# A mixed network of attention, gated linear attention and retention: GpSimd makes the low parts of the weights in the three mixed layers

## The reference

```python
# layer 1
h = rms_norm(x, norm1_g);  proj = h @ w_in
o_attn = dilated_attention(q, k, v, gq, gk)            # 3 groups of 8 heads, merged by their softmax sums
o_gla  = rms_norm(gated_linear_attention(p_q, p_k, p_v, log_a)) * silu(p_r)
x = x + (gate_0 * (o_attn @ w_attn_branch) + gate_1 * (o_gla @ w_gla_branch)) @ w_out
x = x + square(relu(rms_norm(x) @ w_ff_up)) @ w_ff_down
# layer 2: windowed attention with a sink, and neighbourhood attention with a bias table
x = x + concat(window_gqa(...), neighbourhood_attn(...)) @ w_out_e;   x = x + mlp(x)
# layer 3: retention forward and backward, group norm, silu gate
x = x + (silu(g) * group_norm(y_forward + y_backward)) @ w_out_o;     x = x + mlp(x)
```

## Time and profile before

| | us |
|---|---|
| median of 3 runs (2575.36 to 2576.57) | 2576.25 |
| the profiled execution | 2576.55 |
| its span, first to last instruction | 2574.8 |
| PE busy | 2485.3 |
| DVE busy | 1312.8 |
| ACT busy | 934.0 |
| POOL busy | 59.3 |

### The profile page before, as it was taken

One profiled execution on the slowest core, in us unless ns is written; L12 is line 12 of the kernel. 1 busy time (PEld: TensorE's weight loads), 2 busy tenths in 40 slices (PEclk: granted clock), 3 DMA queues, 4 the chain that ended last, 5 costly groups with the idle time before them and its releaser, 6 DMA issues.

```text
span 2574.8 us, 32784 instructions
## 1 busy us (share of the span) xinstructions
PE 2485.3 (97%) x12748; PEld 1949.0 (76%) x12748; DVE 1312.8 (51%) x2065; ACT 934.0 (36%) x1471; POOL 59.3 (2%) x131
## 2 busy tenths in 40 slices
PE   7999999887899999999999999999999999999999
PEld 5777777666788888876576888887677776788887
DVE  4555554665554334447656443345566455634433
ACT  5333453334423223345444332233223232423322
POOL 4000000000000000021000000000000000000000
PEclk9999999998999999999999999999999999999999
DMA  4222213111233333330112333333222221333222
GB/s 140 66 67 66 67 55 94 58 57 43 74 98 99 90 98 103 93 99 25 42 33 74 107 90 98 98 99 89 66 66 82 75 68 41 111 99 107 89 93 78
DMA packets 60640, 205.79 MB, mean 80 GB/s; under 512 B 7249, under 2 KB 7249, under 8 KB 60386
## 3 DMA queue, kind: packets, MB, share of 16 engines
q1 hardware_dynamic: 59760, 202.93, 26.2%
q10 hardware_dynamic: 754, 1.14, 0.1%
HBM read 201.94 MB, written 2.10 MB: 79 GB/s over the span
## 4 chain that ended last, share of the span: by engine, by line
PE 88%; DVE 6%; ACT 4%; issue 1%; POOL 1%; DMA 0%; POOLq 0%; DVEq 0%; ACTq 0%
PE psum L1409 75%; PE psum L1456 2%; PE psum L1492 1%; PE psum L1438 1%; PE psum L1449 1%; PE psum L1434 1%; PE psum L1514 1%; PE psum L1519 1%; PE psum L1484 1%; DVE stage L913 1%; PE psum L1537 0%; ACT tmp L602 0%; DVE arena L1067 0%; ACT tmp L604 0%; PE psum L1504 0%
## 5 line engine op out<-in xcount | busy, mean ns | idle before, releaser
L1409 PE MATMUL psum<-hhi,whi 128*128 128x512 f32 x1640 | 656.7, 400 | 18.1 <-POOL g_mask L501 8.9
L1409 PE MATMUL psum<-hlo,whi 128*128 128x512 f32 x1640 | 666.4, 406 | 0.0
L1409 PE MATMUL psum<-hhi,wlo 128*128 128x512 f32 x1640 | 653.4, 398 | 0.0
L1409 PE MATMUL psum<-uhi,whi 128*128 128x512 f32 x1392 | 555.3, 399 | 7.2 <-DVE hlo L953 2.5
L1409 PE MATMUL psum<-ulo,whi 128*128 128x512 f32 x1392 | 551.4, 396 | 0.0
L1409 PE MATMUL psum<-uhi,wlo 128*128 128x512 f32 x1392 | 547.3, 393 | 0.0
L882 DVE TENSOR_TENSOR wlo<-raw,whi 128x1024 fp32r<-128x1024 f32 (+1 forms) x399 | 465.4, 1167 | 56.1 <-ACT whi L847 29.1
L1409 PEld LDWEIGHTS psum<-hhi,whi 128*128 128x128 f32 x1640 | 313.5, 191 | 88.3 <-POOL g_mask L501 8.9
L1409 PEld LDWEIGHTS psum<-hhi,wlo 128*128 128x128 f32 x1640 | 313.8, 191 | 73.8 <-issue 9.5
L1409 PEld LDWEIGHTS psum<-hlo,whi 128*128 128x128 f32 x1640 | 314.3, 192 | 71.3 <-issue 9.1
L847 ACT CAST whi<-raw 128x1024 fp32r<-128x1024 f32 x190 | 199.6, 1051 | 351.9 <-PE psum L1409 351.9
(11 more groups left out here) (199 smaller groups left out, 1824.5 us busy)
## 6 DMA issues: line engine op xcount, KB each, us to landing
raw<-in_packed_dram SPq DMA_DIRECT2D x359, 512.0 KB, 3.6
raw<-in_packed_dram SPq DMA_DIRECT2D x40, 256.0 KB, 2.6
x<-in_xt_dram SPq DMA_DIRECT2D x8, 256.0 KB, 7.5
out_dram<-x SPq DMA_DIRECT2D x8, 256.0 KB, 2.0
arena<-in_near_bias_dram ACTq DMA_DIRECT2D x1, 1024.0 KB, 5.7
vec<-in_vec_dram ACTq DMA_DIRECT2D x1, 44.0 KB, 4.0
arena<-in_gla_gate_up_dram ACTq DMA_DIRECT2D x1, 32.0 KB
arena<-in_gla_gate_bias_dram ACTq DMA_DIRECT2D x1, 2.0 KB
```

The costliest lines, as they stand in the source:

```text
L1409: mm = pe.matmul(g, w[:, u % 4, k, :], v[:, k, :], start=n == 0, stop=n == 3 * kt - 1)
```

## The change

`split_lo` leaves the mixed layers of DVE. POOL runs it instead, for all units that DVE did in the steps of the three mixed layers and for the two units before the first step: 209 splits, 169 of 1024 columns and 40 of 512. DVE keeps the 142 rows (190 splits, some in loops) of the feed-forward layers. PE waits for `lo_done` as before, now counted up by two engines in turn; for that DVE waits for `lo_done` at the start of each feed-forward layer.

The masks of POOL become functions. `d_pick` is made right behind the constants, without its wait for the first norm. The others stand in a table by unit (`jobs`): at the step of that unit POOL first runs the mask, then the split of u+2. One level of `g_mask` stands at each of the units 2 to 6 of the first layer, the rest of it at unit 7, the dilated mask at 8, the windowed mask at unit 4 of the second layer and all 48 selects of the neighbourhood bias at unit 5.

The first lines that are taken out lie in the steps of the mixed layers, the added wait in the feed-forward layers, the last ones at the start of DVE.

```diff
+            def level_mask(i, m):
...
+            def own_mask():
...
+            def pick():
...
+            def dil_mask():
+                pool.wait_ge(mask_copied, 1)
...
+            def near_mask():
+                pool.wait_ge(rpb_in, 16)
+                within(near_first, near_bias[:, :, 64:256], 8, True)
...
+            def split_lo(u, kt):
+                if u in (first("l2"), first("l3")):
+                    pool.wait_ge(lo_done, u)
+                pool.wait_ge(hi_done, u + 1)
+                pool.tensor_tensor(wlo[:, u % 4, 0:kt, :], raw[:, u % 4, 0:kt, :], whi[:, u % 4, 0:kt, :].bitcast(F32),
+                                   ALU.subtract).then_inc(lo_done, 1)
+            pa = UNIT_OF["copy", "w_in", 0, PA]
+            jobs = {first("l1") + 2 + i: functools.partial(level_mask, i, m) for i, m in enumerate(HALVINGS[2:])}
+            jobs |= {first("l1") + 7: own_mask, first("l1") + 8: dil_mask, pa + 1: ones_row, first("l2") + 4: win_mask, first("l2") + 5: near_mask}
+            pick()
+            split_lo(0, KD)
+            split_lo(1, KD)
+            for name in ("l1", "l2", "l3"):
+                for u, _, _ in steps[name]:
+                    if u is None:
+                        continue
+                    if u in jobs:
+                        jobs[u]()
+                    if not (name != "l1" and u + 2 < first(name) + 2):
+                        split_lo(u + 2, units[u + 2][4])
+                if name == "l1":
+                    distances()
+                if name == "l2":
+                    ret_distance()
...
-                    if u is not None:
-                        split_lo(u + 2, kt=units[u + 2][4])
...
+                dve.wait_ge(lo_done, b + 2)
...
             for k in range(KD):
-                if k == 2:
-                    split_lo(0)
                 squares_after(0, k)
-            split_lo(1)
```

More of the change, by code:

```diff
@@ L1 @@
+import functools
 from contextlib import ExitStack
@@ L502, in _ @@
                                             pattern=[[2 * m, 16 // m], [0, m]], channel_multiplier=-1))
-            for j in range(4):
+            def own_mask():
+              for j in range(4):
                 r = g_mask[32 * j:32 * j + 32, 5, :]
@@ L559, in _ @@
-            within(near_bias, near_bias, 0, False)
-            pool.sem_inc(near_masked, 1)
-            pool.wait_ge(norm_lo, KD * (ORDER["ff1"] + 1))
-            pool.iota(r_dist, pattern=[[1, 7 * P]], base=-3 * P, channel_multiplier=-1,
-                      allow_small_or_imprecise_dtypes=True).then_inc(dist_ready, 1)
+            def pick():
+                done(pool.memset(d_pick, 0.0))
+                v = d_pick[0:4, :].rearrange("p (a b) -> p a b", b=4)
+                done(pool.affine_select(out=v, in_=v, compare_op=ALU.not_equal, fill=1.0, base=0,
+                                        pattern=[[0, P // 4], [-1, 4]], channel_multiplier=1))
+                pool.sem_inc(pick_ready, 1)
@@ new lines, in dil_mask @@
+            def dil_mask():
+                pool.wait_ge(mask_copied, 1)
+                for j in range(4):
+                    r = slice(32 * j, 32 * j + 32)
+                    v = d_bias[r, 0:P]
+                    done(pool.affine_select(out=v, in_=v, compare_op=ALU.is_ge, fill=NEG, base=-j, pattern=[[1, P]],
+                                            channel_multiplier=-4))
+                    v = d_bias[r, P:2 * P]
+                    done(pool.affine_select(out=v, in_=v, compare_op=ALU.is_ge, fill=NEG, base=j, pattern=[[-1, P]],
+                                            channel_multiplier=4))
+                    v = d_bias[r, 256:512].rearrange("p (g l) -> p g l", g=2)[:, :, 96:128]
+                    done(pool.affine_select(out=v, in_=v, compare_op=ALU.is_ge, fill=NEG, base=0, pattern=[[0, 2], [-1, 32]],
+                                            channel_multiplier=1))
+                pool.sem_inc(mask_ready, 1)
@@ new lines, in win_mask @@
+            def win_mask():
+                pool.wait_ge(dist_abs, 1)
+                for sign in (1, -1):
+                    done(pool.affine_select(out=win_dist, in_=win_dist, compare_op=ALU.is_ge, fill=-NEG, base=P - sign * P,
+                                            pattern=[[sign, 3 * P]], channel_multiplier=-sign))
+                pool.sem_inc(dist_pool, 1)
+            def near_mask():
+                pool.wait_ge(rpb_in, 16)
+                within(near_first, near_bias[:, :, 64:256], 8, True)
+                within(near_first[:, :, 128:192], near_first[:, :, 128:192], 24, False)
+                within(near_last, near_bias[:, :, 0:192], 0, False)
+                within(near_last[:, :, 0:64], near_last[:, :, 0:64], 0, True)
+                within(near_bias, near_bias, 0, True)
+                within(near_bias, near_bias, 0, False)
+                pool.sem_inc(near_masked, 1)
```

53 lines of the change are left out of this document (14 added, 39 removed).

## The result

| | before | after |
|---|---|---|
| median, us | 2575.81 (4 runs, 2575.01 to 2576.57) | 2612.36 (4 runs, 2610.43 to 2621.73) |
| ratio to before, 95% interval | | 1.0149 (1.0124 to 1.0174) |
| profiled execution, us | 2576.55 | 2621.73 |
| mean granted clock of the profiled execution | 0.986 | 0.979 |

The change makes the kernel 36.5 us slower, 1.5%. The profiled execution is the longest of the four; the others took 2610 to 2614 us at a clock of 0.982 to 0.984. Lines of the kernel after stand 52 further down in DVE's part (L913 is L965 now) and 47 further down in PE's (L1409 is L1456, L1602 is L1649).

A forecast was written before the change was run, and what follows sets the result against it. PE, busy 2485.3 of 2574.8 us, was taken to set the time. Terms -4.9 + 6.8 + 4 + 2.2 + 10.8 + 10.7 = +29.6 on 2576.55 us gave 2606 us, range 2580 to 2634.

The forecast's parts named there:

- start: Program start: early d_pick removes a 3.54 us wait and the half clock behind, split 1 costs +1.3; together -4.9 us.
- level masks, dilated attention: First layer: splits have two units of lead and miss L1007, so nothing; attention within -2 to +4 us.
- gla heads: Ahead of gla heads 1 to 3 and behind head 3: a split holds DVE's chain, 4 x 1.7 = +6.8 us.
- inside them: Inside the gla heads: splits meet DVE's differences and factors in about two of six units; +4 us, bounds -2 and +10.
- branch: Branch units: two splits hold L949 to L953, DVE's own split goes; 2 x 1.7 - 1.2 = +2.2 us.
- neighbourhood masks: Second layer: unit 7's split queues behind 48 selects; PE waits 8.4 us, then half clock 2.4; +10.8 us.
- retention: Retention heads: splits hold DVE's part 4 chain; 8.5 for five heads, 0.5, 0.8 and 0.9 for others; +10.7 us.
- rival without a hold: POOL does not hold DVE; only start and neighbourhood masks remain, +5.9, 2582 us; chance 0.17.
- rival "faster": The 48 selects end within 22 us, before PE needs unit 7; 2566 us; chance 0.06.
- dear input: The second input makes a POOL split 3.8 us and DVE's hold 3.5; +65, 2642 us; chance 0.14.
- head 4 has a split on the chain now: Retention head 4: a POOL split replaces the DVE split on the chain; 1.7 - 1.2 = +0.5 us.
- Freeing DVE of 209 splits gives PE almost nothing: Mixed layers: DVE's 1.23 us splits mostly lie beside PE's matmuls or ACT's later-ending gate functions, so almost no gain.

The follow-up runs named there:

- e4_all: After, with the edits of e2_near and e3_clear and POOL's split also held back behind part 11 of gla and the branch posts; 2569.16 us, ratio 0.9970.
- e2_near: After, with the neighbourhood bias loaded and its 48 selects run by POOL during the first feed-forward layer; 2604.21 us, ratio 1.0101 to before.
- e3_clear: After, with POOL's split waiting until DVE is through with part 4 of a retention head; 2589.31 us, ratio 1.0051 to before.
- e5_none: e2_near without any split in the mixed layers after the first four units, POOL only counting up (old low parts read); 2560.53 us, ratio 0.9950.
- e1_pick: The kernel before, with only d_pick made ahead of the level masks and all splits kept on DVE; 2570.49 us, ratio 0.9978.
- e8_near_clear: After, with the edits of e2_near and e3_clear but no added waits in gla and at the branch posts; 2581.38 us, ratio 1.0018 to before.
- e9_all_pieces: e4_all, with POOL's split cut into 128-column instructions from the third unit on; 2564.17 us, ratio 0.9957 to before.
- e10_all_256: e4_all, with POOL's split cut into 256-column instructions from the third unit on; 2568.67 us, ratio 0.9966 to before.
- e6_pieces: e2_near, with each POOL split cut into 8 or 4 instructions of 128 columns; 2577.53 us, ratio 1.0008 to before.

## Why the prediction came out right, and which steps did not

The forecast was 2606 us in a range of 2580 to 2634; 2612.4 was measured. Step by step, with the measured terms taken from the traces: PE's 12748 products are the same in every kernel, so each was matched with its like in the kernel before, and a row says how much PE lost in that stretch.

| us of the kernel before | terms | forecast | after | with the cause taken away |
|---|---|---|---|---|
| 0 to 60 | start | -4.9 | -4.9 | |
| 60 to 480 | level masks, dilated attention | 0 | -1.9 | |
| 480 to 740 | gla heads 6.8, inside them 4, branch 2.2 | +13.0 | +15.0 | -0.1 (e4_all) |
| 1145 to 1240 | neighbourhood masks | +10.8 | +12.4 | +0.8 (e2_near) |
| 1240 to 1761 | none | 0 | +0.7 | |
| 1761 to 2300 | retention | +10.7 | +23.9 | -3.3 (e3_clear) |
| sum | | +29.6 | +45.2 | |

The profiled execution of after is the longest of its four; by the medians the change costs 36.5 us, and no trace shows where the other executions are shorter.

**The mechanism was right.** A split holds a DVE instruction until it ends, PE pays where that is on its chain, and the selects hold the split of unit 7. Each of the three losses goes when its cause is taken away, as the last column shows. The rival without a hold falls with the 2.50 us of L1124; the rival "faster" falls with 30.6 us of selects, where it needed 22; the dear input, 3.8 us a split, falls with 2.44.

**The split was mis-sized**, 2.44 instead of 2.0 us, and the hold 2.07 instead of 1.7. The fault was not to take a line up to 1024 columns: the shortest splits, 0.445, 0.717, 1.267 and 2.34 us for 128, 256, 512 and 1024 columns, lie on a line too, with the same 0.17 us at its foot. It was to take the selects' 1.77 ns a column, where the subtraction costs 2.12. The Trainium skill (GPSIMD Engine Reference, section 3.1) would have given 2.25 by half of its 2048-column figure, an estimate that is closer than my line. The gla wait answers to it: 8.92 where I forecast 8.6. The +4 for splits inside the heads was too much: e4_all leaves them there and comes to -0.1 us in that stretch, e5_none, without any, to -2.3, so they are worth some 2 us. The waits ahead of the heads and at the branch, 9.0 forecast, were worth the 15.

**The step that failed is the retention.** The forecast has "head 4 has a split on the chain now: 1.7 - 1.2 = 0.5". I counted one POOL split against the one DVE split. Three came: the casts begun at 2067.11, 2068.68 and 2074.12 each released one, and each took its turn before a DVE instruction. That is +5.0 instead of +0.5, and the last head likewise met three 512-column splits where I counted two. The branch unit has the same error, three splits for two: PE's pause grew by 6.98 - 2.5 = 4.5 us, not 2.2. The second and the third cast had waited for PE to release a buffer, 0.53 and 4.38 us by the trace; a chain that lasts 6 us longer also draws in the next one. With the longer holds PE's pauses in this layer grew by 5 x 2.07 + 5.0 + 0.9 + 2.2 = 18.5 us, not 10.7. The forecast also gave the start and the masks a price for the half clock behind the pause, but none to retention and gla: after the pause of 5.38 us the granted clock is 0.50 for 6.2 us more.

**The freer DVE was taken for nothing.** "Freeing DVE of 209 splits gives PE almost nothing" missed 5.3 us in e4_all and 8.3 in e5_none, both against e1_pick at an equal clock. In the traces the third mixed layer shows it best: it is 2 to 4 us shorter than before in e3_clear, e8_near_clear, e4_all, e5_none, e9_all_pieces and e10_all_256. The branch pause falls from 2.5 to 0.7 us, the wait for the third layer's last `x` from 3.9 to 3.3.

**The masks** were forecast nearly right, +10.8 for 12.4. The levels give only 6.5 us for them, for the reason shown with the fit.

So the retention is short by 13 us, gla and branch by 2 and the masks by 1.6; the median is only 6 us over the forecast. The stretch from 1240 to 1409 us, which holds none of the terms, came out between -7.1 and +4.4 us among the eleven other kernels, with the clock. That the median came so near is in part luck.

## What to carry to other kernels

Before work is moved from DVE to POOL, ask for each piece of it: when is its input ready, and is DVE then in a chain that PE waits for? The price is what is left of POOL's instruction, once for every instruction queued there. A wait that lets POOL start behind the chain (e3_clear, -23 us, in one layer) or shorter instructions (e6_pieces, -27 us) take most of it away; at an equal clock both are worth 21 us. The move paid only with such waits at all three places, by 0.3 to 0.4%, and 0.2% of that is `d_pick` alone, without any split on POOL.

Run times differ by the clock too. Where two variants differ by less than about 10 us of 2570, set their mean clocks beside the times before the edit gets the credit, and match the traces product by product to see in which stretch the difference lies.

## What was not expected of the hardware

- POOL's `tensor_tensor` with two float32 inputs and a rounded output: at the shortest 2.34 us for 1024 columns, 1.27 for 512, 0.72 for 256 and 0.445 for 128. Its copy with one input: 1.08 us on average for 1024.
- Two queues of instructions on DVE and POOL that hold each other go in turn: at the branch post three splits in a row held three DVE instructions, 2.0 to 2.2 us each.
- The mean granted clock of one and the same kernel went from 0.984 to 0.988 between executions (e8_near_clear), and its time from 2585.5 to 2575.7 us.
- At the end of one and the same pause of PE, 1.49 us near 1262 us, the granted clock fell to half in before, e4_all and e10_all_256, and stayed full in e9_all_pieces and e5_none.
